# Six input tiles inside each mLSTM head, and two half output tiles inside the SSD pairs

## The reference

```python
p = h @ w_in                                   # even layer
q, k, v, ig, fg, og, z, xbc, dt = split(p)
# A: mLSTM, 4 heads of 128 keys x 256 values, with a max-stabilised gate
s = einsum(q, k) * w_in;  num = s @ v + (q @ C) * w_prev
C_new = C * decay + (k * g).T @ v
ya = head_norm(num / max(|den|, exp(-m))) * sigmoid(og)
# B: SSD, 16 heads of 64 in 2 groups
xbc = silu(causal_dwconv(xbc));  xs, Bm, Cm = split(xbc)
y  = (C B^T * decay * dt) @ xs + (C @ S) * exp(acum)
yb = rmsnorm_per_group((y + D * xs) * silu(z)) * g
out = concat(ya, yb) @ w_out;  x = x + out
```

## Time and profile before

| | us |
|---|---|
| median of 3 runs | 1053.46 (1052.39 to 1053.93) |
| the profiled execution's own time | 1056.53 |
| its span, first to last instruction | 1054.7 |
| input tiles of the even layer end at | 170.7 |
| mLSTM heads end at | 222.1 |
| first SSD pair's product `sy` starts at | 234.1 |
| tail of the SSD (`sn`) ends at | 301.4 |
| output projection of the even layer ends at | 352.5 |

### The profile page before, as it was taken

How to read it: one execution, slowest core, us unless ns; L and a number is a source line. 1 busy time by engine, 2 the same in 40 slices (tenths; PEclk the granted TensorE clock), 3 DMA queues, 4 the chain that set the end, 5 groups by cost and what they waited for, 6 DMA issues and landing times.

```text
span 1054.7 us, 19149 instructions
## 1 busy us (share of the span) xinstructions
PE 1012.4 (96%) x7256; PEld 945.5 (90%) x7256; DVE 748.1 (71%) x1326; ACT 554.0 (53%) x926; POOL 381.6 (36%) x600
## 2 busy tenths in 40 slices
PE   7999998788999999999999999999979999999996
PEld 7998996454499999999999998999979999999996
DVE  5567589575675899997447856767765599989442
ACT  6346666344155666566444355756644466555431
POOL 4001044232501477775003531232221177777100
PEclk9999998776699999999999999999989999999998
DMA  8635343622445445445544745676644545545541
GB/s 308 239 124 167 130 149 118 221 103 87 142 154 189 165 161 167 173 162 181 169 165 159 261 151 178 200 230 205 191 145 130 182 168 169 171 161 167 189 141 45
DMA packets 64684, 177.22 MB, mean 168 GB/s; under 512 B 5888, under 2 KB 24064, under 8 KB 64592
## 3 DMA queue, kind: packets, MB, share of 16 engines
q1 hardware_dynamic: 64160, 174.14, 49.5%
q0 software_dynamic: 432, 1.85, 0.5%
HBM read 154.92 MB, written 21.05 MB: 167 GB/s over the span
## 4 chain that ended last, share of the span: by engine, by line
PE 86%; DVE 7%; issue 2%; DMA 2%; ACT 2%; POOL 0%; SPq 0%; DVEq 0%; POOLq 0%; ACTq 0%
PE bank L765 24%; PE bank L767 24%; PE bank L766 24%; DVE wl L1528 2%; PE bank L811 2%; DVE cy L1684 1%; DVE E L1884 1%; PE bank L1087 1%; PE bank L823 1%; PE bank L1055 1%; PE bank L832 1%; PE bank L818 1%; PE bank L831 1%; PE bank L877 1%; DMA st<-c_in 1%
## 5 line engine op out<-in xcount | busy, mean ns | idle before, releaser
L1528 DVE TENSOR_TENSOR wl<-raw,wh 128x1024 fp32r<-128x1024 f32 x257 | 315.7, 1232 | 158.2 <-ACT wh L1147 155.5
L1147 ACT ACTIVATE wh<-raw 128x1024 fp32r<-128x1024 f32 x257 | 270.5, 1057 | 288.3 <-PE bank L767 285.2
L765 PE MATMUL bank<-hH,wh 128*128 128x288 f32 x1160 | 349.2, 301 | 7.2 <-DVE wl L1528 6.5
L766 PE MATMUL bank<-hL,wh 128*128 128x288 f32 x1160 | 343.4, 296 | 0.0
L767 PE MATMUL bank<-hH,wl 128*128 128x288 f32 x1160 | 342.6, 295 | 0.0
L765 PEld LDWEIGHTS bank<-hH,wh 128*128 128x128 f32 x1160 | 218.9, 189 | 9.7 <-issue 5.5
L766 PEld LDWEIGHTS bank<-hL,wh 128*128 128x128 f32 x1160 | 219.3, 189 | 0.5
L767 PEld LDWEIGHTS bank<-hH,wl 128*128 128x128 f32 x1160 | 219.5, 189 | 0.0
L1684 DVE SCALAR_TENSOR_TENSOR cy<-pad,vec,cy 128x304 f32<-128x304 f32 (+1 forms) x212 | 145.4, 686 | 4.5 <-ACT cy L1195 0.6
L2056 POOL COPY pad<-fst 128x16 f32<-128x16 f32 x88 | 94.3, 1076 | 66.5 <-DVE cy L1684 66.5
L767 PE MATMUL bank<-HH,wl 128*128 128x288 f32 x352 | 104.3, 296 | 0.0
(11 more groups left out here) (339 smaller groups left out, 1641.7 us busy)
## 6 DMA issues: line engine op xcount, KB each, us to landing
raw<-wts SPq DMA_DIRECT2D x257, 512.0 KB, 3.3
st<-r_in SPq DMA_DIRECT2D x9, 512.0 KB, 7.6
r_out<-st SPq DMA_DIRECT2D x9, 512.0 KB, 4.4
st<-c_in SPq DMA_DIRECT2D x8, 514.0 KB, 5.5
c_out<-st SPq DMA_DIRECT2D x8, 514.0 KB, 3.1
sts<-h_in SPq DMA_DIRECT2D x12, 256.0 KB, 4.7
h_out<-sts SPq DMA_DIRECT2D x12, 256.0 KB, 2.2
st3r<-r_in SPq DMA_DIRECT2D x4, 512.0 KB, 6.3
```

The costliest lines, as they stand in the source:

```text
L765: mm(out, h, xh, start=(k == 0), stop=False)
L766: mm(out, h, xl, start=False, stop=False)
L1147: s.do(act(wh[:, c % RING, :], raw[:, c % RING, :], ACT.Copy), hi_ready)
L1528: do(tt(wl[:, c % RING, :], raw[:, c % RING, :], wh[:, c % RING, :].bitcast(F32), ALU.subtract), lo_ready)
```

## The change

The tiles of the even input are reordered: q, gates, k, then four times (v, v, xbc), which makes 21 tiles (`BODY`). The other 24 tiles are spread over the four mLSTM heads, six to a head (`SPAN`): two xbc, two og, two z. The xbc tiles come with B and C first (`XORDER`). `heads` and `middle` are replaced by functions per step, as the odd layer has them. Sigmoids of og and silus of xbc are run by ScalarE in one place of each head (`gates_and_inputs`), the silus of z in the tail of the SSD. All jobs of the even layer, the SSD pairs among them, use one ring of five banks ("five"), and tiles of the input three. All five state slots are loaded early. In the SSD, the first halves of output tiles 0 and 1 stand in pairs 3 and 4 (`FIRST`), tile 2 among the `su1` updates, tile 3 behind `sn`. The feed-forward's saved rows `fst` are loaded by SyncE after the SSD instead of by GpSimd's queue at the start. The buffers are laid out anew for this.

```diff
-RINGS = {"mix": (4, 5, 6, 7), "low": (0, 1, 2, 3), "odd": (3, 4, 5, 6, 7)}
+RINGS = {"mix": (4, 5, 6, 7), "five": (3, 4, 5, 6, 7)}
...
+            # TensorE
+            for h in range(AH):
+                t = T0 + BODY + SPAN * h
+                tiles([t], operand_of(0))
+                intra_a(h)
+                tiles([t + 1], operand_of(0))
+                chunk_products_a(h)
+                tiles([t + 2], operand_of(0))
+                sample_out_a(h)
+                updates_a(h, range(4))
+                tiles([t + 3], operand_of(0))
+                tiles([t + 4], operand_of(0))
+                updates_a(h, range(4, NB))
+                if h:
+                    back("a", h - 1, h - 1)
+                tiles([t + 5], operand_of(0))
...
+            # ScalarE
+            def step_a(t):
+                split(last_chunk(t) + 3)
+                finish(t - 1)
+            def gates_and_inputs(gates, inputs):
+                for i in gates:
+                    gate_a(i)
+                for n in inputs:
+                    silu_x(n)
+                log_and_exp()
+            for h in range(AH):
+                t = T0 + BODY + SPAN * h
+                step_a(t)
+                gates_and_inputs(...)
+                step_a(t + 1)
+                if h + 2 < AH:
+                    weights("a", h + 2, h + 2)
+                product(f"aoi{h}", num[:, h % 2, 2, 0:AV + 1], cols[:, 2, 32 + h:33 + h])
+                product(f"ao0{h}", num[:, h % 2, 0, 0:AV + 1])
+                if h > 1:
+                    back("a", h - 2, y_even)
+                step_a(t + 2)
+                product(f"ao1{h}", num[:, h % 2, 1, 0:AV + 1])
+                if h:
+                    inverse(h - 1)
...
+                product(f"asp{h}", pout[:, h % 2, 0:AV + 1])
...
+                    s.do(act(vst[row, 0:AV + 1], values_a(h, 2)[0:NS], ACT.Copy), vst_hi)
+                step_a(t + 3)
+                if h + 1 < AH:
+                    keys("a", h + 1, h + 1)
+                step_a(t + 4)
+                step_a(t + 5)
...
+            split(E_OUT + 3)
+            gates_and_inputs((2 * AH - 2, 2 * AH - 1), (XB - 2, XB - 1))
+            eng.wait_ge(tail_done, XB)
+            masked_scores(0)
...
+            back("a", AH - 2, y_even)
...
+            decays(0)
+            decays(1)
+            inverse(AH - 1)
...
+            # VectorE, the last steps of a head
+                step_a(t + 3)
+                sample_out_a(h)
+                updates_a(h, range(4))
+                step_a(t + 4)
+                step_a(t + 5)
+                updates_a(h, range(4, NB))
...
+                # TensorE, SSD pairs
+                if i == 0:
+                    cb(1)
+                if FIRST <= i < FIRST + 2:
+                    out_part("even_out", 0, (i - FIRST,), y_even, (ylo_ready, 0) if i == FIRST else None)
                 sy(i)
...
                 if b == 3:
-                    out_part("even_out", 0, (0,), y_even, (ylo_ready, 0))
-            out_part("even_out", 0, (1,), y_even)
+                    out_part("even_out", 0, (2,), y_even)
...
-            out_part("even_out", 0, (2, 3), y_even)
+            out_part("even_out", 0, (3,), y_even)
```

More of the change, by code:

```diff
@@ L145, in tile @@
         phase = TILES[t][0]
-        use(t, (t - START[phase]) % (3 if phase == "odd" else 4))
+        use(t, (t - START[phase]) % (3 if phase in ("even", "odd") else 4))
     def out_tail(phase):
@@ L194, in plan_banks @@
-        job(f"aos{h}", "dve")
-        for b in range(NB):
-            job(f"ass{h}.{b}", "dve", "low")
+            job(f"abc{h + 2}", "act", "five")
+        job(f"aoi{h}", "act", "five")
+        job(f"ao0{h}", "act", "five")
+        tile(T0 + BODY + SPAN * h + 1)
+        job(f"ao1{h}", "act", "five")
+        job(f"asp{h}", "act", "five")
+        if h + 1 < AH:
+            front("a", h + 1, "five")
+        tile(T0 + BODY + SPAN * h + 2)
+        job(f"aos{h}", "dve", "five")
+        for b in range(4):
+            job(f"ass{h}.{b}", "dve", "five")
@@ L197, in plan_banks @@
+        tile(T0 + BODY + SPAN * h + 3)
+        tile(T0 + BODY + SPAN * h + 4)
+        for b in range(4, NB):
+            job(f"ass{h}.{b}", "dve", "five")
         if h:
-            turned_back("a", h - 1, "low")
-    for name in ("cb0", "cb1", "bn0", "bn1", "sbc0", "sbc1"):
-        job(name, "act")
+            turned_back("a", h - 1, "five")
+        tile(T0 + BODY + SPAN * h + 5)
+    for name in ("cb0", "bn0", "bn1", "sbc0", "sbc1"):
+        job(name, "act", "five")
     for i in range(3):
-        job(f"xn{i}", "dve", "low")
@@ L203, in plan_banks @@
-    turned_back("a", AH - 1, "low")
+        job(f"xn{i}", "dve", "five")
+    turned_back("a", AH - 1, "five")
     for i in range(PAIRS):
@@ L240, in plan_banks @@
         if t == O + LEAD - 2:
-            front("r", 0, "odd")
-            job("rv0", "dve", "odd")
-    job("rv1", "dve", "odd")
+            front("r", 0, "five")
+            job("rv0", "dve", "five")
+    job("rv1", "dve", "five")
     for h in range(CH):
@@ L886, in back @@
                     turn_back(f"{kind}yt{2 * h + i}", lambda g: num[:, hg % 2, g, i * P:(i + 1) * P])
-            def heads(kind, n, first, qk, va, w):
-                for h in range(n):
-                    if kind == "a" and 2 < h + 2 < n:
-                        row_max(h + 2)
-                    middle(kind, h, first + h, lambda g: va(g, h), w, (lambda: front(kind, h + 1, qk)) if h + 1 < n else None)
             def ffn(l):
@@ L1414, in _, with decays @@
-            for h in range(BH):
+                s.do(act(cbm[g][:, 0:TP + P], b[:, 0:TP + P], ACT.Copy))
+                s.do(act(cbm[g][0:NS, TP + P:BLK], b[0:NS, TP + P:BLK], ACT.Copy), mix_act)
+            def decays(h):
                 wait_job(eng, f"sbc{h}")
@@ L1835, in xn @@
+            evacuate(START["even_out"] - 1)
+            split(E_OUT + 3)
+            back("a", AH - 2)
+            statistics("a", AH - 1, AH - 1)
+            normalise("a", AH - 1, AH - 1)
             def xn(i):
```

601 lines of the change are left out of this document (312 added, 289 removed).

## The result

| | before | after | predicted |
|---|---|---|---|
| median, us | 1053.53 (1052.39 to 1053.93) | 1071.55 (1070.89 to 1072.16) | 1058.2 (1044 to 1067) |
| span of the profiled execution | 1054.7 | 1070.4 | 1059.4 |
| its own time | 1056.53 | 1072.16 | 1061.2 |

The change makes the kernel slower by 1.8%: ratio 1.0177, 95% interval 1.0164 to 1.0191. The sign was forecast, the size was not: 18.0 us where 4.7 were expected, and the time lies 4.5 us above the range. So totals are compared by medians and stages by the traces.

A forecast was written before the change was run, and what follows sets the result against it. It took the mLSTM heads as bound by latency and clock, the SSD pairs by TensorE at half clock. Terms -24.2 - 3.2 + 14.6 + 4.5 + 6.8 + 4.2 + 2.0 = +4.7 gave 1058.2 us, range 1044 to 1067.

The forecast's parts named there:

- Part 1: mLSTM heads: with six tiles each, the heads' own work takes 27.2 us in place of 51.4, -24.2 us.
- The gate rows and the body: Body: gate rows move from behind tile 16 to behind tile 4, about 0.8 of the stall stays, -3.2 us.
- Part 2: Head groups: new TensorE waits from the order of the lists and the ring of five banks, +14.6 us.
- (a): Heads 0 to 2: fourth update waits 1.85 us each for the bank ScalarE's `keys` empties, 5.6 us.
- (b): Heads 1 to 3: turn back waits 2.05 us each for VectorE to empty a bank, longer beside `kgm`, 8.2 us.
- R1: Rival, heads: groups run dense without the new waits, as in the retention group; 1039.1 us, chance 0.14.
- The clock: Heads: three of six or seven waits lower TensorE's clock, 1.5 us each, +4.5 us; bounds 0 and 10.5.
- Part 3: Start of the SSD: ScalarE's work behind the last tile, with three table loads, delays `inverse` and `normalise`, +6.8 us.
- R4: Rival, ScalarE: table changes drain it first, another 1.37 us each, three times; 1062.3 us, chance 0.04 together with another rival.
- Part 4: SSD pairs 3 and 4, and tail: moved half output tiles cost +4.2 us in the pairs and +2.0 in the tail.
- R2: Rival: waits stay, but tiles keep the clock up through the SSD's first three pairs; 1050.6 us, chance 0.13.
- R3: Rival: every one of seven waits drops the clock (+6.0), `cb1` at half clock (+1.7), ring +1; 1066.9 us, chance 0.19.

The follow-up runs named there:

- clean kernel: Changed kernel with keys and updates early, table blocks at the heads' ends, three body edits, and half output tiles back in their old places: 1032.4 us, ratio 0.9800.
- keys early: Changed kernel with ScalarE's keys of the next head ahead of the high part of chunk t+6: 1066.8 us.
- values later: Changed kernel with the body's value tiles reordered so that the first turn of values comes one tile later: 1074.7 us.
- the body's three on the changed kernel: Changed kernel with fourth tile on bank 7, first turn of values one tile later, and state loads between the weights: 1069.4 us.
- updates early: Changed kernel with VectorE's updates 4 to 7 ahead of the low part of chunk t+8: 1060.5 us.
- both: Changed kernel with ScalarE's keys ahead of the weights and VectorE's updates 4 to 7 ahead of the low part: 1054.9 us, ratio 1.0012.
- block in head 3: Changed kernel with the last two sigmoids and silus and three table loads moved from behind the heads into head 3: 1071.55 us.
- bank: Changed kernel with the fourth tile of the even input projection on bank 7: 1072.1 us.
- the three with the blocks moved and the half tiles in the pairs: Changed kernel with early keys and updates and table blocks at heads' ends: 1043.4 us; plus state loads between weights: 1043.6; plus two more body edits: 1037.9.

## Why the prediction was right or wrong

**Part 1, the tiles (-24.2): right, to 1 us.** But it shows only in a kernel without the waits, at 105.0 for priced 104.0. The retention group was the right yardstick.

**The gate rows and the body (-3.2): wrong by 5.7.** The step that failed is "no og tile, no sigmoid and no turned value stands in this chain, so about 0.8 stays". It counted what left the chain and didn't ask who comes next. (If nothing of the 3.2 came, the record names that bound, 0; the other 2.5 had no term.) Timeline of the kernel after, VectorE, then TensorE:

```profile
52.14 0.30 DVE L1813 TENSOR_SCALAR slab<-rows 4x288 f32<-4x288 f32 x1 [2.33 <-ACT rsm L1355]
```

```profile
24.82 0.61 PE L807 MATMUL bank<-hH,wh 128*128 128x288 f32 x1 [1.56 <-DVE qT L1634]
...
55.81 0.55 PE L853 MATMUL bank<-cst,vT 128*128 128x128 f32 x3 [2.50 <-DVE vT L1634]
```

VectorE still waits 2.33 for ScalarE's exponentials, and the first value tile, whose turn stands one tile behind it, is evacuated behind the backlog. Further, the diff lets the even tiles go round three banks, not four, and the record never priced that for tile 3, which now waits for the first evacuation behind the norm: 1.56 at 24.8. In this trace 3.4 us at half clock lie beside it (24.4 to 27.8); eight other traces have the same wait and no such stretch there, but 3.4 to 6.9 us at half clock before 18.5, so that stretch isn't shown to be the wait's doing. With both waits mended (1.0 for `kT` comes in their place) the first head product came 4.0 us earlier (90.0 to 86.0) in the kernels that had the loads between the weights.

**Part 2, the waits (+14.6): right in place and in sum (15.8).** (a) was priced 1.85 each and measured 1.2 to 1.6 (4.2 for 5.6). (b) was priced 8.2 and measured 8.4, with 3.2 us in the two heads where GpSimd's `kgm` lies beside the low part, which then takes 2.14 (149.9 us). Head 3's wait for `vst` was priced 0.8; the two on "issue" cost 3.2, since in head 2 too the table loads hold ScalarE back ahead of `vst`. R1 was wrong: the retention group's order doesn't carry over.

**The clock (+4.5): the mechanism right, the size wrong.** "I take three, since most are shorter than that row's" failed, and so did the 1.5 us for each. In the heads with their tiles 24 us ran at 1.2 GHz, in five stretches: three of 3.4 us and two of 6.8, each beside a wait or within 2 us of one; the first two waits (1.60 and 1.42) had none. By the stage table the heads exceed their clean 105.0 by 26.3, of which 15.8 are waits: 10.5 are left for the clock, 6.0 more than priced and just the upper bound that the record named and didn't take. In the clean kernel waits of 1.59 us did it twice in three. This is the largest miss.

**Part 3 (+6.8): right within 1.2.** Timeline of VectorE in the kernel after:

```profile
240.13 1.06 DVE L1705 TENSOR_SCALAR num<-num,mv,sm 128x256 f32<-128x256 f32 x3
```

`normalise` starts 12.4 after the heads' end (227.7), as forecast (12.5). The table loads took 1.28 each with the next instruction 1.29 behind, three in a row, so the rule of the Trainium skill (ScalarE: Activation LUTs, What ACT_TABLE_LOAD costs; 2.66 us a switch) is not borne out here either, and R4 falls. The step that failed is the 0.95 taken off: from the start of `normalise` to `sy0` pass 7.5 us, before 7.0.

**Part 4 (+4.2 and +2.0): the right price, for another clock than this kernel had.** From `sy0` to the norm 118.4 us passed before, and the sum said 124.6. All kernels with the half tiles in the pairs, by the time at 1.2 GHz in that stretch:

| at 1.2 GHz | `sy0` to norm | kernels |
|---|---|---|
| 29.3 | 120.6 to 120.8 | after, keys early, values later, the body's three on the changed kernel |
| 38.5 | 122.4 | updates early, both |
| 47.2 to 47.6 | 124.4 to 124.7 | block in head 3, bank, the three with the blocks moved and the half tiles in the pairs |

So 18 us more at half clock cost 4.0 here, a quarter and not a half. VectorE bounds part of the pairs when the clock is high: TensorE waits 3.0 us for its `E` in the kernel after and 0.7 in the kernel with the block in head 3. The forecast assumed the low level throughout, which the kernels of the last line show. In the changed kernel part of the low time fell into the start of the part, where TensorE idled anyway (clock 0.62). That is a piece of R2, but by where the slow time falls, not by the tiles. Undone, part 4 gave 4.0 in the changed kernel and 5.5 in the clean kernel; from `sy0` to the norm their traces give 2.2 (120.7 to 118.5) and 7.1 (124.4 to 117.3). TensorE's idle time ahead of `sn` came as priced (4.4 for 4.7), and `sn` then took 6.5 us where it took 4.1 before, the fall of the clock that the record names:

```profile
313.19 6.46 PE L1095 MATMUL bank<-xbcT,cst 128*128 128x288 f32 x16 [4.43 <-ACT xbcT L1519]
```

**R3**, every wait drops the clock, was the rival that came nearest (1066.9). With the body's 5.7 it would have been 1072.6. Of those 5.7, 3.2 were a bound that the record names ("if the stall stays as it is, 0") and did not carry into the range, and 2.5 were in no case; so the range ended at 1067. To the letter R3 was wrong: the clock fell at five places of seven, for longer at two of them, and that the measured 1071.5 lies so near 1072.6 is partly luck, since part 4 cost 3.9 us less.

**Readings of the record that don't hold.** The low slices before are those from 158 to 290 us, not 185 to 317. The 51.1 us hold 14 half output tiles and the first two up tiles; the price of 3.2 each stays. In part 1, 7.8 less twice 0.3 is 7.2 and not 7.1, which makes 27.6 for the heads' own work and 104.4 for the 104.0 that 105.0 is compared with.

## What to carry to other kernels

When dense work is put between latency-bound steps, count every short wait with its length and with the slow stretch that follows; here 4.8 us of waits cost 8.7. Look on each in-order engine for the instruction that needn't be late (the keys behind a weight, four updates behind a low part, a table block ahead of `vst`), and mend them together: alone, the table block, the bank and the order of the loads won nothing that can be told, and the later values lost 3 us, because the next wait, slower pairs, or stretches at half clock elsewhere took it. Four such orders, a bank, an order of loads and the old place of the half tiles turned a change that cost 1.8% into one that wins 2.0% over the kernel before.

## What the runs showed of the hardware

Loads of saved state issued in one row held the next weights up: ScalarE waited 8.25 us for them while the queue carried five transfers of 514 KB, and in that time the DMA engines were full (share 1.03, 415 GB/s), though over the body they are used to 0.55 on average.

The clock is no function of the wait's length alone. Of three waits of 1.59 us at the same place of three heads two were followed by 3.4 us at 1.2 GHz and one was not; with the keys early a wait of 3.21 us (181.0 us in that trace) was followed by none.

And a trace can't show a gain of 1 or 2 us in the body: seven kernels with the same body reach the first head product between 89.3 and 92.4 us, with 3.4 to 10.2 us at 1.2 GHz before it.
